# Unread products ahead of the first projection, attention scores two heads ahead, and the last norm and store by halves, in a kernel of two transformer blocks

## The reference, cut to what matters

```python
def second_block(x, mem, ...):
    x = x + 0.5 * swiglu_ffn(rms_norm(x, ffn1_norm[l]), ...)
    h = rms_norm(x, mix_norm[l])
    ...
    o_a = indexed_sparse_attention(q_a, k_a, v_a, ...) @ w_o_a[l]   # 8 heads
    ...
    o_m = memory_attention(q_m, m_k, m_v) @ w_o_m[l]                # 4 heads
    merged = g[:, :, 0] * o_a + g[:, :, 1] * o_b + g[:, :, 2] * o_m
    x = x + merged @ w_out[l]
    x = x + 0.5 * swiglu_ffn(rms_norm(x, ffn2_norm[l]), ...)
    return rms_norm(x, final_norm[l])

def rms_norm(x, g):
    return x * rsqrt(mean(x * x, -1) + NORM_EPS) * g
```

## Time and profile before

| | us |
|---|---|
| median of three runs | 2177.38 |
| the three runs | 2173.64 to 2178.76 |
| the profiled execution | 2174.22 |
| its span, first to last instruction | 2172.4 |
| PE busy | 2119.5 (98%) |
| DVE busy | 1595.0 (73%) |
| ACT busy | 1215.9 (56%) |
| mean granted TensorE clock | 0.991 |

### The profile page before, as it was taken

One profiled execution on the slowest core, in us unless ns is written; L12 is line 12 of the kernel. 1 busy time (PEld: TensorE's weight loads), 2 busy tenths in 40 slices (PEclk: granted clock), 3 DMA queues, 4 the chain that ended last, 5 costly groups with the idle time before them and its releaser, 6 DMA issues.

```text
span 2172.4 us, 31475 instructions
## 1 busy us (share of the span) xinstructions
PE 2119.5 (98%) x11887; PEld 1770.4 (81%) x11887; DVE 1595.0 (73%) x1654; ACT 1215.9 (56%) x1204; POOL 171.3 (8%) x240
## 2 busy tenths in 40 slices
PE   8999999999899999999999999999999999999998
PEld 7987888898778788888888888888788887877886
DVE  3677454577788989989898989989866539776453
ACT  4254443415467777777777777777664423664442
POOL 1200000310200000000000000000166010000000
PEclk9999999999999999999999999999999999999999
DMA  9224555422589999999999999999846564435552
GB/s 353 70 98 165 186 186 184 142 66 93 177 325 373 351 371 375 357 377 360 372 362 371 360 376 367 363 375 362 317 155 192 183 182 156 155 107 173 180 188 78
DMA packets 244114, 542.21 MB, mean 250 GB/s; under 512 B 20182, under 2 KB 122624, under 8 KB 243648
## 3 DMA queue, kind: packets, MB, share of 16 engines
q1 hardware_dynamic: 238608, 521.37, 66.5%
q0 software_dynamic: 4448, 13.79, 2.4%
q10 hardware_dynamic: 976, 5.91, 0.7%
HBM read 538.64 MB, written 2.36 MB: 249 GB/s over the span
## 4 chain that ended last, share of the span: by engine, by line
PE 83%; DVE 10%; issue 3%; ACT 2%; DMA 2%; DVEq 0%; SPq 0%; ACTq 0%
PE bank L1334 9%; PE bank L1335 9%; PE bank L1336 9%; PE bank L1489 7%; PE bank L1485 7%; PE bank L1486 7%; PE bank L1060 6%; PE bank L1512 4%; PE bank L1513 4%; PE bank L1517 4%; DVE weights_lo L2443 2%; PE bank L1058 2%; PE bank L1647 2%; DMA ring_data<-in_moe_w 1%; PE bank L1473 1%
## 5 line engine op out<-in xcount | busy, mean ns | idle before, releaser
L2443 DVE TENSOR_TENSOR weights_lo<-ring_data,weights_hi 128x2048 fp32r<-128x2048 f32 x336 | 760.0, 2288 | 84.4 <-ACT weights_hi L2124 83.2
L2124 ACT ACTIVATE weights_hi<-ring_data 128x2048 fp32r<-128x2048 f32 x336 | 639.0, 1919 | 178.6 <-DMA ring_data<-in_moe_w 178.1
L1485 PE MATMUL bank<-weights_hi,xg_hi 128*128 128x512 f32 x896 | 352.5, 393 | 2.6 <-DVE arena L2901 2.6
L1486 PE MATMUL bank<-weights_hi,xg_lo 128*128 128x512 f32 x896 | 349.8, 390 | 0.0
L2438 DVE TENSOR_TENSOR weights_lo<-ring_data,weights_hi 128x2048 fp32r<-128x2048 f32 x98 | 228.2, 2358 | 49.3 <-ACT weights_hi L1899 49.3
L1489 PE MATMUL bank<-weights_lo,xg_hi 128*128 128x512 f32 x896 | 240.2, 390 | 0.5 <-DVE weights_lo L2443 0.5
L1335 PE MATMUL bank<-weights_lo,xT_hi 128*128 128x512 f32 x584 | 229.5, 393 | 0.0
L1334 PE MATMUL bank<-weights_hi,xT_hi 128*128 128x512 f32 x520 | 206.2, 397 | 1.6 <-issue 0.6
L1336 PE MATMUL bank<-weights_hi,xT_lo 128*128 128x512 f32 x520 | 203.1, 391 | 0.0
L1485 PEld LDWEIGHTS bank<-weights_hi,xg_hi 128*128 128x128 f32 x896 | 168.6, 188 | 37.1 <-issue 3.0
L1489 PEld LDWEIGHTS bank<-weights_lo,xg_hi 128*128 128x128 f32 x896 | 168.5, 188 | 36.3 <-DVE weights_lo L2443 1.0
(11 more groups left out here) (522 smaller groups left out, 3184.0 us busy)
## 6 DMA issues: line engine op xcount, KB each, us to landing
ring_data<-in_moe_w SPq DMA_DIRECT2D x672, 512.0 KB, 4.4
ring_data<-in_ffn_w_in SPq DMA_DIRECT2D x88, 512.0 KB, 4.5
ring_data<-in_w_in SPq DMA_DIRECT2D x71, 512.0 KB, 4.3
ring_data<-in_ffn_w SPq DMA_DIRECT2D x66, 512.0 KB, 4.0
ring_data<-in_ffn_w_out SPq DMA_DIRECT2D x44, 512.0 KB, 4.0
ring_data<-in_w_out SPq DMA_DIRECT2D x24, 512.0 KB, 4.6
ring_data<-in_w_in SPq DMA_DIRECT2D x8, 396.0 KB, 4.0
ring_data<-in_w_in SPq DMA_DIRECT2D x8, 390.0 KB, 5.4
```

Of the source, the lines that this page charges most:

```text
L1485: mm(o, xg_hi[:, k, :], e_hi(at)[:, r], start=k == 0, stop=False)
L1486: mm(o, xg_lo[:, k, :], e_hi(at)[:, r], start=False, stop=False)
L2124: nc.scalar.activation(e_hi(at), ring_data[:, e_slot(at), :], ACT.Copy).then_inc(ring.hi_done, 1)
L2443: v.tensor_tensor(e_lo(at), ring_data[:, e_slot(at), :], e_hi(at), ALU.subtract).then_inc(ring.lo_done, 1)
```

## The change

1. PE, ahead of its wait for the input: 7 products of a 128 x 128 by a 128 x 256 part of `sigb` into bank 7, which nobody reads. DVE clears `sigb` first, as its first step, and PE waits for that step.
2. The loop over the heads issues `scores(h + 2)` where it issued `scores(h + 1)`.
3. The last norm and store by halves. A root of `mem_ss` that nobody reads stands ahead of the squares on ACT. Each half of 512 features is squared on its own; the first half's sum, divided by D and with NORM_EPS added by DVE, is the bias of the tile's root. DVE's adds, factors and scalings of the two tiles are interleaved, and SP stores four halves.
4. The signal of the number of passes is counted by `dve_stage` instead of by a semaphore of its own, for SP (shown), POOL, PE, ACT and DVE alike.

```diff
-    ("mem_factor", "router_max", "sel_ready", "norm_rows2", "pcol_ready", "lambda_inverse", "row_factor_m", "mk_sumsq", "mk_normed", "blocks_out", "states_ready", "keys_chosen", "heads_sumsq", "heads_normed", "u_split"),
+    ("mem_factor", "router_max", "sel_ready", "norm_rows2", "npass_ready", "pcol_ready", "lambda_inverse", "row_factor_m", "mk_sumsq", "mk_normed", "blocks_out", "states_ready", "keys_chosen", "heads_sumsq", "heads_normed", "u_split"),
...
+        ss_half, eps_half = ssq[:, 0:2 * TT].rearrange("p (j q) -> p j q", j=TT), rq[:, 0:TT]
...
-            sp.wait_ge(sem("npass_ready"), 1)
+            sp.wait_ge(sem("dve_stage"), stage("npass_ready"))
...
             for j in range(TT):
-                sp.wait_ge(sem("x_done"), j + 1)
-                sp.dma_start(out[0, P * j:P * j + P, :], x[:, j, :]).then_inc(sem("out_stored"), 16)
-            sp.wait_ge(sem("out_stored"), 16 * TT)
+                for q in range(2):
+                    sp.wait_ge(sem("x_done"), 2 * j + q + 1)
+                    sp.dma_start(out[0, P * j:P * j + P, 512 * q:512 * q + 512], x[:, j, 512 * q:512 * q + 512]).then_inc(sem("out_stored"), 16)
+            sp.wait_ge(sem("out_stored"), 32 * TT)
...
                 if l == 0:
+                    pe.wait_ge(sem("dve_steps"), 1)
+                    for _ in range(7):
+                        mm(bank[7][:, 0:T], sigb[:, 0, 0:P], sigb[:, 1, :], start=True, stop=True)
                     pe.wait_ge(sem("xT_loaded"), 16)
...
                 for h in range(AH + MH):
-                    if 1 < h + 1 < AH + MH:
-                        scores(h + 1)
+                    if h + 2 < AH + MH:
+                        scores(h + 2)
                     turn_p(h)
...
-            rms(3, x, (sem("x_fed"), TT + 1), tiles=True)
+            a_(mem_r[:, :], mem_ss[:, :], ACT.Sqrt, "act_steps", scale=1.0 / D, bias=NORM_EPS)
+            for j in range(TT):
+                for q in range(2):
+                    c = slice(512 * q, 512 * q + 512)
+                    act.wait_ge(sem("x_mixed"), 4 + 2 * j + q + 1)
+                    a_(hbuf[:, j, c], x[:, j, c], ACT.Square, "rms_sq", accum_out=ss_half[:, j, q:q + 1])
+                act.wait_ge(sem("rms_sq"), 3 * TT + 2 * j + 2)
+                act.wait_ge(sem("eps_ready"), j + 1)
+                a_(r2[:, j:j + 1], ss_half[:, j, 1:2], ACT.Sqrt, "rms_std", scale=1.0 / D, bias=eps_half[:, j:j + 1])
...
                 if l == 0:
+                    st.do(v.memset(sigb[:, :, :], 0.0))
                     st.do(v.memset(qkv_raw[:, :, 0:3], 0.0))
...
-            fed(ffn2, 2)
+            dense(ffn2, 2)
             dve.wait_ge(sem("pool_fetched"), 64)
-            dve.wait_ge(sem("rms_std"), 4)
-            st.do(v.reciprocal(r2[:, :], r2[:, :]))
-            st.settle()
-            for j in range(TT):
-                v.scalar_tensor_tensor(x[:, j, :], x[:, j, :], r2[:, j:j + 1], final_g, ALU.mult, ALU.mult).then_inc(sem("x_done"), 1)
+            def fed_half(j, q):
+                xs = x[:, j, 512 * q:512 * q + 512]
+                bank_done(ffn2, 2, 2 * j + q)
+                v.scalar_tensor_tensor(xs, bank[2 * j + q][:, :], 0.5, xs, ALU.mult, ALU.add).then_inc(sem("x_mixed"), 1)
+            def half_squares(j):
+                dve.wait_ge(sem("rms_sq"), 3 * TT + 2 * j + 1)
+                v.tensor_scalar(eps_half[:, j:j + 1], ss_half[:, j, 0:1], 1.0 / D, NORM_EPS, ALU.mult, ALU.add).then_inc(sem("eps_ready"), 1)
+            def factor(j):
+                dve.wait_ge(sem("rms_std"), 4 + j)
+                st.do(v.reciprocal(r2[:, j:j + 1], r2[:, j:j + 1]))
+                st.settle()
+            def scaled_half(j, q):
+                c = slice(512 * q, 512 * q + 512)
+                v.scalar_tensor_tensor(x[:, j, c], x[:, j, c], r2[:, j:j + 1], final_g[:, c], ALU.mult, ALU.mult).then_inc(sem("x_done"), 1)
+            fed_half(0, 0)
+            fed_half(0, 1)
+            half_squares(0)
+            fed_half(1, 0)
+            half_squares(1)
+            factor(0)
+            scaled_half(0, 0)
+            fed_half(1, 1)
+            scaled_half(0, 1)
+            factor(1)
+            scaled_half(1, 0)
+            scaled_half(1, 1)
```

More of the change, by code:

```diff
@@ L920, in _ @@
             pool.wait_ge(sem("pool_fetched"), 32)
-            pool.wait_ge(sem("npass_ready"), 1)
+            pool.wait_ge(sem("dve_stage"), stage("npass_ready"))
             last = pool.value_load(npass_i[0:1, 1:2], min_val=E - 1, max_val=2 * E - 1)
@@ L1575, in moe @@
                     up_slot(0, m, m, FFN_LOADS + m + 1)
-                pe.wait_ge(sem("npass_ready"), 1)
+                pe.wait_ge(sem("dve_stage"), stage("npass_ready"))
                 last = pe.value_load(npass_i[0:1, 1:2], min_val=E - 1, max_val=2 * E - 1)
@@ L2129, in moe @@
                     a_(ex[:, j], lgt[:, j], ACT.Exp, "router_exp", bias=m1[:, j:j + 1])
-                act.wait_ge(sem("npass_ready"), 1)
+                act.wait_ge(sem("dve_stage"), stage("npass_ready"))
                 last = act.value_load(npass_i[0:1, 1:2], min_val=E - 1, max_val=2 * E - 1)
@@ L2857, in moe @@
                 st.settle()
-                v.tensor_copy(npass_i[:, :], cnt[:, 1:3]).then_inc(sem("npass_ready"), 1)
-                dve.wait_ge(sem("npass_ready"), 1)
+                v.tensor_copy(npass_i[:, :], cnt[:, 1:3]).then_inc(sem("dve_stage"), 1)
+                dve.wait_ge(sem("dve_stage"), stage("npass_ready"))
                 last = dve.value_load(npass_i[0:1, 1:2], min_val=E - 1, max_val=2 * E - 1)
```

## The result

The changed kernel takes 2165.43 us (median of 6 runs, 2165.07 to 2169.80), the kernel before 2177.81 (6 runs, 2173.64 to 2178.76): 12.4 us less. The ratio estimated from all runs is 0.9948, 95% interval 0.9936 to 0.9959, which is 8.9 to 13.9 us. The forecast was 2171.4, 2167.5 to 2176.0. A second set of runs on another chip repeats it: 2165.14 against 2177.86 (0.9943, 0.9930 to 0.9956, which is 9.6 to 15.2 us). One execution in all, of the kernel that starts late, was slow (2867 us at a mean granted clock of 0.699) and is left out of every figure.

The account below looks back on a forecast made before the run. TensorE (PE) holds 83% of the chain, so edits pay only where PE stands still, runs slowly, or behind its last product. 1.6 + 2.0 + 2.4 = 6.0 us saved; 2168.2 for the profiled execution, 2171.4 as median, range 2167.5 to 2176.0.

Parts of the forecast that it names:

- Part 1: Start: unread products on PE during the DMA wait let the first projection run at the upper clock level; 1.6 us saved.
- rival (a): Start: the pause before 8.24 us lets the clock fall, so the unread products give nothing; 2173.0 us, chance 0.22.
- 2.0 is nearer to the pause that held: Start: clock expected to hold over the 2.0 us pause, since it held after 1.68 and fell after 2.34 and 2.57.
- part 2: Attention of block 2: scores issued two heads ahead, so the loop of waits no longer binds; 2.0 us saved, bounds 0.8 to 2.9.
- Rival (b): Attention: scores two ahead only move the wait to DVE's scaling or ACT's copies; 0.8 instead of 2.0, 2172.6 us, chance 0.09.
- part 3: End: last norm and store by halves, table load off the path; 2.4 us saved, bounds 1.0 to 3.2.
- Rival (c): End: the square needs its own table, so loads of 1.28 us come between squares and roots; 2174.5 us, chance 0.07.
- 1.64 saved ... I take 1.6: Start: first projection takes 5.61 us instead of 7.25 if the upper clock level holds; counted as 1.6 us.
- The median of the three runs is 3.2 above that execution; against it, 2171.4: Whole kernel: profiled execution's forecast of 2168.2 us raised by the distance from that execution to before's median.
- the lower end of the range: Whole kernel: 2167.5 us, from a best case of 2168.8 and earlier runs 3.7 below their median.
- Rival (d): Behind 8.24 us: shifted work makes the clock fall at pauses where it held, 1.7 us each; six falls 2181.6, chance 0.07.
- low at more places than now: Whole kernel: the prediction called itself wrong if the granted clock were low at more places than before; no size given.

Follow-up runs that it names:

- the kernel that starts late: Kernel before, with PE also waiting for the next weights ahead of its first projection, no products added; 2180.64 us, ratio 1.0006.
- the eight cold profiles above: Profiles starting the first projection at the lower clock: five of before, three of before with only the scores, only the end, or both changed; average 112.59 us at one load.
- the three looks: Three more profiled executions of the unchanged kernel before; they took 2180.19, 2178.59 and 2179.70 us.
- part 1 alone: Kernel before plus only the seven unread products and their memset; 2171.16 us, ratio 0.9972; on a second chip 2169.38 us, 0.9966.

## Why the prediction missed, by its own steps

**Right: what bounds the kernel, and where the edits act.** All three places did as described. Part 1's passes ended at 6.78 (forecast near 6.2), and the clock was held over the pause: rival (a) is out, with pauses of 1.05, 1.14 and 1.40 us, and in the first profile of part 1 one of 2.10, as long as the one weighed. The reason given, that 2.0 is nearer to the pause that held, isn't borne out: in the stage of the experts the clock fell behind pauses of 1.87 and 1.92 us (last section). The Trainium skill says ("TensorE: Matmul & The Clock Gate", Part 1: The HAM clock gate) that the point of change varies from run to run. The traces bear this out: 7.01 to 8.55 us for one and the same projection. The prediction named this and gave it no weight in the sum.

**Right: part 2.** 2.0 forecast, 2.3 measured (bounds 0.8 and 2.9); the 2.64 in the trace of after hold the 0.36 of part 1. With the 0.19 us by which the trace of after is later there, the transposes of heads 7, 8 and 9 stand at 1901.5, 1903.4 and 1905.3 on before's scale; forecast were 1901.6, 1903.4 and 1905.4. Rival (b) is out.

**Right: part 3.** 2.4 forecast, 2.0 and 2.2 measured. On before's scale the last half add ends at 2164.5 (forecast 2164.65) and the last scaling at 2167.25 (2167.2); the data end 0.3 later than forecast, since the last two stores flow for 1.6 us instead of 1.3. A square with its read takes 0.73 us from start to end (2157.09 to 2157.82; the read starts before the square's row ends), 0.72 was taken. Rival (c) is out: four squares and two roots follow one load. (The price given for (c) is too low by its own terms: three loads of 1.28 behind the first half adds are 3.84, which puts part 3 at +1.4 instead of +0.7.) The Trainium skill ("ScalarE: Activation LUTs", Table sets) lists relu, copy, identity and abs as in every set; square is used here without a load as well.

**Wrong: the price of part 1, "1.64 saved ... I take 1.6".** It was read from one execution, which was among those with the shortest cold start. The first projection takes 7.0 to 8.6 us cold, so 1.4 to 2.9 are saved there; and the executions above before's median also lose 1.0 to 2.2 us between 57 and 111 us, in the fall at 54 us. At the load near 111 us the eight cold profiles above that have no products average 112.59, the four with seven products 109.35: 3.2 us; the three looks average 113.81: 4.5. Before ran 114 times beside the experiments, and 67 of these took more than 2176.5 us; if the looks stand for them, the median lies among them, and 4.5 is the term for it.

**Wrong for the same reason: "The median of the three runs is 3.2 above that execution; against it, 2171.4".** The offset was carried over as if the change didn't touch it. It is in part what the change takes away: before's runs in its second set spread over 9.6 us (2170.3 to 2180.0), part 1's on the same chip over 3.8 and the change's over 2.9 (12, 6 and 5 runs). Part 1's first set has 8.5, by one run at 2177.5; the next is 2173.9. The sum with 4.5 in place of 1.6 is 8.9, and against the median of before 2168.9, inside the range and still 3.5 above what was measured.

**Wrong: the lower end of the range.** Its best case was 2168.8, and it named runs 3.7 us below their median; taken off whole, that gives 2165.1, which would have held the result. 2167.5 takes off 1.3, without a reason.

**Rival (d)**, and the sign "low at more places than now": by the two first traces it came, six places against five up to PE's last product. But the sixth, at 429 us, is in four of the five profiles of before as well, and over many executions the change has no more low clock than before: the mean granted clocks of the five runs of its second set are 0.991 to 0.992, of the 18 of before beside them 0.988 to 0.993. What (d) had against it, that the pauses keep their lengths, is wrong: the one at 752 us, 1.68 us there, is 0.19 in the second profile of part 1 and 1.92 in the change with twelve products.

**What stays open.** 12.4 us were measured and the traces place 4.5 + 2.3 + 2.1 = 8.9 of them, which is the lower end of the first interval and below that of the second (9.6). The rest, some 3 us, must lie behind 111 us: from there to the end, less parts 2 and 3, the five profiles of before are 1.3 us longer on average than its first and the four with seven products 1.8 shorter, but single ones scatter by 4 to 6 us. Of these 3.1 us, 0.36 are the ones of part 1 from 1886 to 1920 us, and 2.5 lie in the stage of the experts, which takes 963.9 us on average in the five and 961.5 in the four. Low clock explains little of it: all have 3.4 us of it there, the third look 6.8. What differs is PE's wait for an add of DVE: 1.7 to 3.9 us in sum in the five, 0.2 to 2.7 in the four. Waits from 609 to 1563 us in the first trace of before and from 607 to 1557 in the second profile of part 1:

```profile
PE bank L1463 <- DVE arena L2895: 3.6, 7, 1.7
...
PE bank L1466 <- DVE arena L2899: 0.2, 1, 0.2
```

The pause of before at 752.12 us shows the chain behind it. ACT waits for weights from DMA, DVE for ACT's half of them, and the add stands behind DVE's work on them:

```profile
746.62 1.92 ACT L2124 ACTIVATE weights_hi<-ring_data 128x2048 fp32r<-128x2048 f32 x1 [3.13 <-DMA ring_data<-in_moe_w]
748.58 2.29 DVE L2443 TENSOR_TENSOR weights_lo<-ring_data,weights_hi 128x2048 fp32r<-128x2048 f32 x1 [0.75 <-ACT weights_hi L2124]
750.78 1.28 DVE L2895 TENSOR_TENSOR arena<-arena,bank 128x512 f32<-128x512 f32 x2
```

In that profile of part 1, ACT's longest wait for DMA at this place is 1.09 us. Whether the seven products bring this about, or nine profiles are too few to average it out, these runs don't tell; the kernel with three products, which starts cold, has the shortest stage of all, 960.0 us. Low-clock stretches come and go too: those near 190, 430, 754, 1366 and 1950 us are there in one execution and not in the next, those near 570 and 1570 are always there and last 6.8 to 13.7 us. Why a longer cold start and the fall at 54 us go together isn't shown either, only that they do.

## What to carry to other kernels

A cold start's price is a distribution: look at several profiled executions, above all one from above the median, before pricing an edit that removes it. Where runs of one kernel scatter by more than the edit is worth, ask which of the edit's steps acts on the scatter, and don't add the distance from the profiled execution to the median as a constant. Count filler at the start by whether the next real work starts at the upper level, not by how early it starts: three products gave nothing, and seven and twelve the same in part 1 alone.

## What the runs showed of the hardware that was not expected

The granted clock can fall while PE has no pause at all: in seven of the 18 profiles from a point between 52 and 59 us on and, in the second layer, from a point between 429 and 437 us on in most profiles, during or right behind 24 products of two columns and 48 of 64 x 64, with PE busy for 1.00 of every window shown. It was low for 3.4 or 6.8 us there. With six products of 256 columns among the sparse ones it did not fall in the one profile taken.

How long a pause was didn't decide by itself whether the clock fell behind it. It held over 2.10 us ahead of the first projection (part 1 alone) and over 1.68 in the stage of the experts, and fell behind 1.87 us there in the third look at before and behind 1.92 in the change with twelve products:

```profile
752.91 0.50 PE L1468 MATMUL bank<-Y_hi,chosen 128*128 128x512 f32 x1 [1.92 <-DVE arena L2909]
...
753.00:754.00 1.00, 1.00 (x5) 1.00 0.94 340
754.00:755.00 1.00, 1.00 (x5) 0.67 0.94 377
```

The clock column reads 1.00 for the first low stretch of an execution, in every profile; only the pace of the passes shows it (7.25 us against 5.61).
